# Scaling the probabilities of layer 1's attention on GpSimd instead of VectorE

## The chip, the cores and the metric

The kernel runs on one core of a Trainium2 chip, in one launch. The metric is the device time of a run in microseconds; lower is better. The core has TensorE (matrix products; the profile shows its weight loads as a unit of their own, PEld), VectorE (DVE), ScalarE (ACT), GpSimd (POOL) and SyncE (SP), each with its own stream of instructions, which meet in semaphores.

## The reference

The reference runs two blocks of two layers each over 256 positions of width 1024, with a second stream of 256 context positions in the first block. What matters here is layer 1 of the first block, a sliding-window attention with 16 query heads of 64 channels, 4 key heads, a context and a sink:

```python
def one_block(j):
    ...
    s_loc = jnp.einsum('bqkgd,bskd->bkgqs', q_blk, k_blk,
                       preferred_element_type=jnp.float32) * scale
    s_loc = jnp.where(valid, s_loc, NEG_INF)
    s_ctx = jnp.einsum('bqkgd,bckd->bkgqc', q_blk, kc,
                       preferred_element_type=jnp.float32) * scale
    s = jnp.concatenate([s_loc, s_ctx, s_sink], axis=-1)
    p = jax.nn.softmax(s, axis=-1).astype(v.dtype)
    return (jnp.einsum('bkgqs,bskd->bqkgd', p[..., :3 * T], v_blk)
            + jnp.einsum('bkgqc,bckd->bqkgd', p[..., 3 * T:3 * T + C], vc))
```

The softmax divides each row of exponentials by its sum; here that is done before the product with the values. Around it stand the normalisations, the projections, squared-ReLU layers of width 4096, and in the second block a state-space layer and a second attention.

## The kernel before

The whole network is one program with a function per engine. Most of the time goes into large products (`gemm` on TensorE, L730 to L732: three products for each pair of operands split into a high and a low part), whose weights SyncE loads in units of 512 KB. The stages stand one behind the other in every engine's program, in the same order: q1, k1, v1 of layer 1, its attention, its output projection wo1, and so on.

Layer 1's attention (`ATT1`) has 16 groups, each of two heads and 128 queries against 512 keys (256 positions and 256 of context). Group g uses two of four score banks, two of four `prob` tiles (g % 2 selects them) and one of four columns of `stat`, the small tile with maximum, sum, inverted sum and sink term. The steps of one group n are:

- scores (TensorE, L914): two heads, 64x128 against 64x512, into banks;
- mask (VectorE, L2120): the window, 256 keys wide, is added in the banks; maximum (L2121, a reduction over 128x1024); then two short steps for the sink (L2127, L2128);
- exponentials (ScalarE): L1436 for the sink term, L1440 twice into `prob`, each with a read of the accumulated row sum;
- sum (VectorE, L2136: row sum plus sink term), reciprocal (L2137), and the scaling of both heads' `prob` tiles in place (L2140, 128x512 f32 twice);
- transposes (TensorE, L925): four per head, each head once its tile is scaled;
- copy (ScalarE, L1427): both heads' transposed probabilities from the banks into `prob_t`;
- values (TensorE, L940): 16 small products into a bank; every second group its output goes to `u_hi` (ScalarE, L1448) and `u_lo` (VectorE, L2148).

The order on each engine is written out in its `attention` function. In step n TensorE does the scores of n+1, the transposes of n-1 and the values of n-2. VectorE does mask and maximum of n (`att_max`), sum, reciprocal and scaling of n-1 (`att_scale`), and the low part of the output of n-3. ScalarE does the copy of n-2, the output of n-3 and the exponentials of n. The scores of a group wait until the exponentials of the group two before it, which used the same banks, are done. The semaphore `att_r` counts scaled tiles: VectorE raises it after each head, and TensorE waits for it before that head's transposes. Layer 0's attention (`ATT0`) runs through the same functions with 32 groups, without sink and window, and its first 16 groups have the same shapes on TensorE.

GpSimd does no arithmetic here beyond a few memsets at the start. It issues DMAs: the rotated copies of queries and keys ahead of layer 1's attention (L2352), and behind it, once wo1's units are through, the table loads of `table_inputs` (L2316 to L2318) for the second block. Between the two it has nothing to do during layer 1's attention.

Of the kernel before, what the change touches and what calls it, by code (L numbers as in the profile page):

```python
# [7 lines left out]
ALU = mybir.AluOpType  # L8
# [9 lines left out]
TOK = 2 * SEQ  # L18
# [136 lines left out]
def program(nc, weights, ada_w, ada_b, x_t, vecs, cons, bias_na, ssm_in, ssm_bc, scratch, out):  # L155
# [5 lines left out]
    with ctx:  # L161
# [4 lines left out]
        def place(name, shape, dt=F32, at=None):  # L166
            size = int(np.prod(shape[1:])) * 4
            off = cursor[0] if at is None else at
            if at is None:
                cursor[0] += (size + 31) // 32 * 32  # L170
            return nc.alloc_sbuf_tensor_at(name, shape, dt, offset=off)
# [51 lines left out]
        prob = place("prob", [P, 4, TOK], at=at_)  # L223
# [4 lines left out]
        stat = place("stat", [P, 4, 4, 2], at=rsn_at)  # L228
# [85 lines left out]
        def sem(name):  # L314
            return ctx.enter_context(nc.semaphore(name))
# [34 lines left out]
        att_s, att_m, att_p, att_r, att_t, att_e, att_o, att_h, att_l = (sem("att_" + c) for c in (  # L350
            "scores", "max", "probs", "scaled", "transposed", "probs_t", "out", "out_hi", "out_lo"))
# [13 lines left out]
        ge_y, ge_t, ge_a, ge_sg, ge_g, ge_hi, ge_lo = (sem("gelu_" + c) for c in (  # L365
            "input", "square", "argument", "sigmoid", "product", "out_hi", "out_lo"))
        h_out = sem("h_out")

        block = ctx.enter_context(nc.Block())

        def value(name, s, n):

            return n + (CREDIT + s.base.get(name, 0))

        def stage_end(eng, s, names):

            inc = increments(s)
            for n in names:
                if n in inc:
                    eng.wait_ge(S[n], CREDIT + s.base.get(n, 0) + inc[n])  # L380

        class Chain:
# [13 lines left out]
            def link(self, ins):  # L396
                self.until(self.mark(ins))
# [44 lines left out]
        for s in ST.values():  # L442
            a = s.base.get("ada_read", 0)
# [71 lines left out]
        ATT0, ATT1 = [], []  # L515
# [1046 lines left out]
        def _(dve):  # L1562
# [445 lines left out]
            while n < CH:  # L2008
                b = [p_[:, n, :].unsqueeze(1).to_broadcast([P, n, PAIRS]) for p_ in (pr_, pi_)]
# [120 lines left out]
            def att_scale(groups, m, base):  # L2130
                _, keys, _, _, kind, _ = groups[m]
                g = m + base
                b = g % 4
                dve.wait_ge(att_p, 2 * g + 2)
                if kind == "swa":
                    link(TT(stat[:, 1, b, :], stat[:, 1, b, :], stat[:, 3, b, :], ALU.add))  # L2136
                link(dve.reciprocal(stat[:, 2, b, :], stat[:, 1, b, :]))  # L2137
                for a in range(2):
                    pb = prob[:, 2 * (g % 2) + a, 0:keys]
                    TS(pb, pb, stat[:, 2, b, a:a + 1], None, ALU.mult).then_inc(att_r, 1)  # L2140
# [140 lines left out]
        def _(pool):  # L2281
# [63 lines left out]
            for n, (name, done) in enumerate((("q1", 4), ("q1", 8), ("k1", 2))):  # L2345
                pool.wait_ge(S["d2"], value("d2", ST[name], done))
                if n == 0:
                    stage_end(pool, ST["down0b"], ("d1",))
                for p0 in range(0, P, 16):
                    p1 = p0 + 16 if p0 % 32 == 0 else p0 - 16  # L2350
                    src_ = q1[p1:p1 + 16, 4 * n:4 * n + 4, :] if n < 2 else k1[p1:p1 + 16, :, 0:SEQ]
                    pool.dma_start(turned[p0:p0 + 16, 4 * n:4 * n + (4 if n < 2 else 2), :], src_).then_inc(rope_in[n], 16)  # L2352
            stage_end(pool, ST["wo1"], ("unit",))
            table_inputs(HOME1, slice(PAIRS // 2, PAIRS))
            for n in range(4, PIECES):
# [169 lines left out]
```

## Time and profile before

| | |
|---|---|
| Median of 3 runs | 1713.21 us (1707.87 to 1715.15) |
| Span of the profiled execution | 1706.6 us |
| TensorE busy | 1606.4 us, 94% |
| Weight loads (PEld) busy | 1421.1 us, 83% |
| VectorE busy | 1308.7 us, 77% |
| ScalarE busy | 869.5 us, 51% |
| GpSimd busy | 104.3 us, 6% |
| Mean granted TensorE clock | 0.982 |

The profile is one execution, traced by the hardware; its span runs from the first to the last instruction. Times in the rows are microseconds from the span's start, durations are microseconds unless marked ns. Each instruction has its line in the kernel, and where its engine stood idle before it, the idle time and who ended it stand in square brackets. The ends of TensorE's instructions are modelled, so their starts say more than their durations. An arrow reads "written from".

### The profile page before, as it was taken

To read this page: it belongs to the slowest core of one execution; us is meant where nothing else is said; L and a number is where in the kernel's file an instruction comes from. 1 tells how busy PE (TensorE), PEld (TensorE's weight loads), DVE (VectorE), ACT (ScalarE), POOL (GpSimd) and SP (SyncE) were. 2 spreads that over 40 slices of the span, in tenths; PEclk is the share of its full clock that TensorE was granted. 3 is DMA by queue.
4 is the path that set the end of the run, shared out by engine and by line. 5 is a ranking of instruction groups with operands and counts; after the bars stand their busy time and mean duration, and the time that the engine had idled before them with its cause. 6 is when DMAs were issued, how large, how long until landed. Compare 5 with 4: busy or idle time off the path is not lost.

```text
span 1706.6 us, 32698 instructions
## 1 busy us (share of the span) xinstructions
PE 1606.4 (94%) x11872; PEld 1421.1 (83%) x11872; DVE 1308.7 (77%) x2229; ACT 869.5 (51%) x1505; POOL 104.3 (6%) x174
## 2 busy tenths in 40 slices
PE   6999899899999999788989999889999999899999
PEld 3778666688888888674789999789999998699999
DVE  5899897788767867678677787777887686578874
ACT  4664386343213433566555555355555586555542
POOL 0001030000000023120000212000000000000000
PEclk9999999999999999998999999999999999999999
DMA  9246651345667855340156667735555644055554
GB/s 368 89 137 224 218 149 51 123 144 184 202 193 238 263 173 169 112 140 12 53 186 202 217 208 263 316 102 176 179 183 177 205 153 158 13 164 183 182 196 137
DMA packets 80828, 292.02 MB, mean 171 GB/s; under 512 B 10432, under 2 KB 12224, under 8 KB 78928
## 3 DMA queue, kind: packets, MB, share of 16 engines
q1 hardware_dynamic: 69552, 249.03, 44.4%
q0 software_dynamic: 11168, 41.54, 7.6%
q8 instruction: 69, 1.13, 0.3%
q14 instruction: 39, 0.32, 0.1%
HBM read 270.54 MB, written 18.68 MB: 169 GB/s over the span
## 4 chain that ended last, share of the span: by engine, by line
PE 73%; DVE 18%; issue 4%; ACT 3%; DMA 2%; ACTq 0%; DVEq 0%; SPq 0%; POOLq 0%
PE bank L730 22%; PE bank L732 21%; PE bank L731 21%; DVE stat L2121 2%; DVE w_lo L1576 2%; DVE prob L2140 1%; PE bank L914 1%; DVE bank L1588 1%; DVE ada_raw L1589 1%; PE bank L925 1%; DMA raw<-weights 1%; PE bank L940 1%; DVE qk L1771 1%; DMA ada_raw<-ada_w 1%; PE bank L818 1%
## 5 line engine op out<-in xcount | busy, mean ns | idle before, releaser
L730 PE MATMUL bank<-u_hi,w_hi 128*128 128x256 f32 (+1 forms) x1936 | 615.9, 318 | 31.2 <-DVE u_lo L1951 19.2
L731 PE MATMUL bank<-u_lo,w_hi 128*128 128x256 f32 (+1 forms) x1936 | 600.8, 310 | 0.0
L732 PE MATMUL bank<-u_hi,w_lo 128*128 128x256 f32 (+1 forms) x1936 | 600.8, 310 | 0.0
L1576 DVE TENSOR_TENSOR w_lo<-raw,w_hi 128x1024 fp32r<-128x1024 f32 x372 | 452.2, 1222 | 143.9 <-ACT w_hi L1144 131.4
L1144 ACT ACTIVATE w_hi<-raw 128x1024 fp32r<-128x1024 f32 x360 | 375.4, 1049 | 172.8 <-PE bank L732 142.7
L730 PEld LDWEIGHTS bank<-u_hi,w_hi 128*128 128x128 f32 x1936 | 372.5, 192 | 59.6 <-issue 35.7
L731 PEld LDWEIGHTS bank<-u_lo,w_hi 128*128 128x128 f32 x1936 | 372.8, 193 | 22.3 <-issue 3.8
L732 PEld LDWEIGHTS bank<-u_hi,w_lo 128*128 128x128 f32 x1936 | 372.6, 192 | 18.4
L730 PE MATMUL bank<-hid_hi,w_hi 128*128 128x512 f32 (+1 forms) x512 | 174.0, 340 | 0.0
L732 PE MATMUL bank<-hid_hi,w_lo 128*128 128x512 f32 (+1 forms) x512 | 172.1, 336 | 0.0
L731 PE MATMUL bank<-hid_lo,w_hi 128*128 128x512 f32 (+1 forms) x512 | 172.0, 336 | 0.0
L730 PEld LDWEIGHTS bank<-hid_hi,w_hi 128*128 128x128 f32 x512 | 97.1, 190 | 11.0 <-issue 1.5
L732 PEld LDWEIGHTS bank<-hid_hi,w_lo 128*128 128x128 f32 x512 | 97.1, 190 | 10.2
L731 PEld LDWEIGHTS bank<-hid_lo,w_hi 128*128 128x128 f32 x512 | 97.1, 190 | 9.7
L1589 DVE SCALAR_TENSOR_TENSOR ada_raw<-ada_raw,silu_row 128x1024 f32<-128x1024 f32 x80 | 97.7, 1222 | 9.3 <-DMA ada_raw<-ada_w 9.0
L730 PE MATMUL bank<-f_hi,w_hi 128*128 128x256 f32 x352 | 99.8, 283 | 0.0
L731 PE MATMUL bank<-f_lo,w_hi 128*128 128x256 f32 x352 | 99.6, 283 | 0.0
L732 PE MATMUL bank<-f_hi,w_lo 128*128 128x256 f32 x352 | 99.6, 283 | 0.0
L1195 ACT ACTIVATE rs<-bank 128x512 f32<-128x512 f32 (+1 forms) x64 | 31.3, 489 | 125.2 <-PE bank L732 118.7
L730 PEld LDWEIGHTS bank<-f_hi,w_hi 128*128 128x128 f32 x352 | 67.6, 192 | 0.2
L732 PEld LDWEIGHTS bank<-f_hi,w_lo 128*128 128x128 f32 x352 | 67.6, 192 | 0.0
L731 PEld LDWEIGHTS bank<-f_lo,w_hi 128*128 128x128 f32 x352 | 67.6, 192 | 0.0
(317 smaller groups left out, 2260.3 us busy)
## 6 DMA issues: line engine op xcount, KB each, us to landing
raw<-weights SPq DMA_DIRECT2D x372, 512.0 KB, 3.4
ada_raw<-ada_w SPq DMA_DIRECT2D x80, 512.0 KB, 4.1
ada_first<-ada_w SPq DMA_DIRECT2D x16, 512.0 KB, 14.4
bias_sb<-bias_na POOLq DMA_DIRECT2D x16, 256.0 KB, 3.4
toep_dram<-zeros POOLq DMA_DIRECT2D x8, 512.0 KB, 9.1
bat_dram<-bat POOLq DMA_DIRECT2D x16, 256.0 KB, 4.2
ca_dram<-ca POOLq DMA_DIRECT2D x16, 256.0 KB, 3.8
s_bat<-bat_dram POOLq DMA_DIRECT2D x4, 1024.0 KB, 8.2
```

The lines of the kernel that those rows point to most:

```text
L730: pe.matmul(dst, wh, hi[:, kt, xs], start=first, stop=False)
L731: pe.matmul(dst, wh, lo[:, kt, xs], start=False, stop=False)
L732: return pe.matmul(dst, wl, hi[:, kt, xs], start=False, stop=final)
L818: pe.matmul(SUM_BANKS[b2][:, 0:s.tok], C("block"), sq[:, b2, 0:s.tok], start=True, stop=True).then_inc(S["p2"], 1)
L914: pe.matmul(psum[2 * (g % 2) + a][:, 0:keys], q_ap, k_ap, start=True, stop=True).then_inc(att_s, 1)
L925: mm = pe.transpose(psum[4 + a][:, t * P:(t + 1) * P], prob[:, 2 * (g % 2) + a, t * P:(t + 1) * P], C("ident"))
L940: mm = pe.matmul(psum[6 + pr % 2][a * HD:(a + 1) * HD, qt * P:(qt + 1) * P], heads[a][2][t], prob_t[:, 2 * (g % 2) + a, t * P:(t + 1) * P] ...
L1144: A(w_hi[:, slot, :], raw[:, slot, :], ACT.Copy).then_inc(S["hi"], 1)
L1195: chain.link(A(rs[:, b2, 0:s.tok], bank[:, 0:s.tok], ACT.Relu))
L1576: TT(w_lo[:, slot, :], raw[:, slot, :], w_hi[:, slot, :].bitcast(F32), ALU.subtract).then_inc(S["lo"], 1)
L1589: STT(raw_, raw_, 1.0, silu_row[:, 0, :], ALU.mult, ALU.mult, accum_out=ada_acc[:, b, a % 4, 0:1]).then_inc(S["ada_read"], 1)
L2121: red = dve.tensor_reduce(stat[:, 0, b, :], both[:, :, 0:keys], AX.X, ALU.max, negate=True)
```

## The change

After the reciprocal, VectorE's part of a group ends in layer 1 with a raise of a new semaphore `att_v`. GpSimd waits for it once per group, and then does the two scalings in place, with the same operands as VectorE had, and raises `att_r`. VectorE no longer waits for its own reciprocal there. Layer 0's attention stays as it was. In GpSimd's program the sixteen groups stand behind the DMAs of the rotated keys and ahead of the wait for wo1.

```diff
+        att_v = sem("att_sums_inverted")
...
                 if kind == "swa":
                     link(TT(stat[:, 1, b, :], stat[:, 1, b, :], stat[:, 3, b, :], ALU.add))
+                if kind == "swa":
+                    dve.reciprocal(stat[:, 2, b, :], stat[:, 1, b, :]).then_inc(att_v, 1)
+                    return
                 link(dve.reciprocal(stat[:, 2, b, :], stat[:, 1, b, :]))
                 for a in range(2):
                     pb = prob[:, 2 * (g % 2) + a, 0:keys]
...
+            for m in range(len(ATT1)):
+                g = m + len(ATT0)
+                pool.wait_ge(att_v, m + 1)
+                for a in range(2):
+                    pb = prob[:, 2 * (g % 2) + a, 0:TOK]
+                    pool.tensor_scalar(pb, pb, stat[:, 2, g % 4, a:a + 1], None, ALU.mult).then_inc(att_r, 1)
             stage_end(pool, ST["wo1"], ("unit",))
```

## Rows read from the trace of the kernel before

**Rows 1.** The page: the chain that ended last, shares of the span by engine and line.

```profile
PE 73%; DVE 18%; issue 4%; ACT 3%; DMA 2%; ACTq 0%; DVEq 0%; SPq 0%; POOLq 0%
PE bank L730 22%; PE bank L732 21%; PE bank L731 21%; DVE stat L2121 2%; DVE w_lo L1576 2%; DVE prob L2140 1%; PE bank L914 1%; DVE bank L1588 1%; DVE ada_raw L1589 1%; PE bank L925 1%; DMA raw<-weights 1%; PE bank L940 1%; DVE qk L1771 1%; DMA ada_raw<-ada_w 1%; PE bank L818 1%
```

**Rows 2.** Stretches of layer 1's attention: length, busy per engine, clock, DMA share, GB/s.

```profile
772.00:784.00 12.00, 9.81 (x26) 3.92 (x27) 8.23 (x21) 5.13 (x15) 0.00 (x0) 0.51 0.00 1
784.00:828.00 44.00, 40.00 (x360) 25.66 (x358) 40.69 (x110) 34.30 (x84) 0.00 (x0) 1.00 0.01 1
```

**Rows 3.** Timeline, layer 1's attention: start, duration, engine, line, operation, [idle before].

```profile
786.01 0.15 DVE L2136 TENSOR_TENSOR stat<-stat 128x2 f32<-128x2 f32 x1
...
789.26 0.15 DVE L2136 TENSOR_TENSOR stat<-stat 128x2 f32<-128x2 f32 x1
789.38 0.20 ACT L1436 ACTIVATE stat<-stat 128x2 f32<-128x2 f32 x1
789.45 0.17 DVE L2137 RECIPROCAL stat<-stat 128x2 f32<-128x2 f32 x1
...
789.65 0.88 DVE L2140 TENSOR_SCALAR prob<-prob,stat 128x512 f32<-128x512 f32 x2
...
790.19 1.09 PE L925 MATMUL bank<-con,prob 128*128 128x128 f32 x8
...
790.72 0.20 ACT L1440 ACTIVATION_READ_ACCUMULATOR prob<-bank,stat 128x1 f32 x1
...
791.22 1.09 PE L940 MATMUL bank<-prob_t,val 128*64 128x128 f32 x16
...
792.24 1.13 PE L914 MATMUL bank<-k,q 64*128 64x512 f32 x4
...
794.03 0.42 DVE L2120 TENSOR_TENSOR bank<-bank,con 128x256 f32<-128x256 f32 x1
...
796.10 0.15 DVE L2136 TENSOR_TENSOR stat<-stat 128x2 f32<-128x2 f32 x1
```

**Rows 4.** Timeline, layer 0's attention: GpSimd released by VectorE's maximum.

```profile
210.72 1.23 DVE L2121 TENSOR_REDUCE stat<-bank 128x2 f32<-128x1024 f32 x1
...
212.24 0.84 POOL L2304 DMA_DIRECT2D bias_sb<-bias_na  x1 [2.44 <-DVE stat L2121]
```

**Rows 5.** Waits from 784 to 828: who waited for whom, us, times, longest.

```profile
PEld bank L925 <- DVE prob L2140: 12.5, 12, 1.2
```

**Rows 6.** Timeline of TensorE in layer 0's attention: scores of two groups in succession.

```profile
211.82 1.13 PE L914 MATMUL bank<-qk 64*128 64x512 f32 x4
...
214.92 1.13 PE L914 MATMUL bank<-qk 64*128 64x512 f32 x4
```

**Rows 7.** GpSimd's memsets by line and form: count | busy us, mean ns | idle.

```profile
L2284 POOL MEMSET zeros<- 128x128 f32 x1 | 0.2, 223 | 0.0
L2512 POOL MEMSET const-float32-1.0<- 128x1 f32 x1 | 0.1, 99 | 0.0
```

**Rows 8.** Timeline, the last groups: sum and transposes of the last but one, its copy.

```profile
827.16 0.16 DVE L2136 TENSOR_TENSOR stat<-stat 128x2 f32<-128x2 f32 x1
...
828.10 1.09 PE L925 MATMUL bank<-con,prob 128*128 128x128 f32 x8 [1.47 <-DVE prob L2140]
...
829.28 1.02 ACT L1427 ACTIVATE prob_t<-bank 128x1024 f32<-128x1024 f32 x1 [0.46 <-issue]
```

**Rows 9.** Timeline: scores at the lower clock, and the mask that waited for them.

```profile
781.79 2.08 PE L914 MATMUL bank<-k,q 64*128 64x512 f32 x4
...
783.94 0.43 DVE L2120 TENSOR_TENSOR bank<-bank,con 128x256 f32<-128x256 f32 x1 [0.57 <-PE bank L914]
```

**Rows 10.** Timeline: the first group's sum and its transposes.

```profile
778.55 0.15 DVE L2136 TENSOR_TENSOR stat<-stat 128x2 f32<-128x2 f32 x1
...
779.89 1.97 PE L925 MATMUL bank<-con,prob 128*128 128x128 f32 x8
```

**Rows 11.** Timeline of GpSimd: its first instruction after layer 1's attention.

```profile
858.57 0.74 POOL L2316 DMA_DIRECT2D tab_bbar<-bbar_dram  x1 [92.41 <-PE bank L732]
```

## The prediction

> **What bounds the kernel now.** I read the page first. TensorE is busy for 94% of the span and holds 73% of the chain that ended last, nearly all of it in the big products of L730 to L732; VectorE's share of that chain is 18%, and one of its entries is L2140, the line that the change moves [rows 1]. An edit to VectorE pays only where the chain runs through VectorE, so I went to the one stage touched. By the busy times of three stretches, layer 1's attention has a start of 12 us with TensorE at a granted clock of 0.51, its lower level (1.2 GHz), after it had waited for the rotated keys, and then 44 us at 1.00 (2.4 GHz), in which VectorE is busy 40.69 us and GpSimd 0.00 [rows 2].
>
> The timeline of two consecutive groups shows the order [rows 3]. VectorE's sum of group n (L2136) starts at 789.26, the same instruction two groups on at 796.10: 6.84 us for two groups, 3.42 for one. From the sum that starts at 786.01 (group 2) to that of group 14 at 827.16 it is 41.15 us for twelve groups [rows 3, 8]: 3.43 each. In the table of waits TensorE's weight loads for the transposes (L925) wait 12.5 us for L2140 in this stretch [rows 5]. So VectorE sets the pace, and TensorE is close behind. How close shows layer 0's attention, whose later groups have the same shapes on TensorE: there scores start at 211.82 and the next scores at 214.92, and TensorE waits for nobody [rows 6]. That is 3.10 us per group, TensorE's own floor. Twelve groups at 3.10 are 37.2 us, so no version of this change that leaves TensorE alone can give back much more than 41.15 - 37.2 = 3.9 us, 0.23% of the run. The forecast lives or dies on whether GpSimd costs that little.
>
> **What is removed.** Per group two scalings on VectorE, 0.88 us together, from 789.65 [rows 3], and the short wait between the reciprocal and them. 16 groups x 0.88 = 14.1 us of VectorE time. VectorE's occupied time per group falls from 3.43 to about 2.5 us. That is not the gain, since the floor of 3.10 is late next, and since the scaled probabilities still have to be made before the transposes.
>
> **What is added.** Two scalings of 128x512 f32 on GpSimd, and a hop from VectorE to GpSimd. No row shows GpSimd doing arithmetic. The nearest are its two memsets: one element per partition takes 0.10 us, 128 elements 0.22 us [rows 7]. That is (0.223 - 0.099) / 127 = 0.98 ns per element, so 512 elements written cost 0.10 + 0.50 = 0.60 us by this slope. An operation that also reads can hide the reading under the writing (0.60) or do one after the other (0.10 + 1.00 = 1.10). I estimate 0.75 us for one scaling, T below: nearer to the memset, as it is the same engine with the same size of element, plus something for the read and the per-partition factor. If a third pass came in (reading, multiplying, writing, nothing overlapped), T would be 0.10 + 1.50 = 1.6; I keep 0.6 and 1.6 as the ends.
>
> The hop: where GpSimd waited for VectorE's maximum, the reduction ended at 211.95 and its next instruction began at 212.24, 0.29 us later; that one issues a DMA [rows 4]. VectorE's products reach TensorE within 0.10 (first scaling done near 790.09, transposes at 790.19) [rows 3]. I take 0.20 for the way in, between the two, and 0.10 for the way out.
>
> The Trainium skill, "GPSIMD Engine Reference", section Performance versus the Vector engine, gives one measured loop of 512 elements at 769 ns, and calls elementwise work on VectorE the rule, as GpSimd needs about twice its time. No trace here shows that figure yet; by it the result would be 0.3 us above my sum, and the rule speaks against this change.
>
> **The loop that carries the cost.** TensorE's order is written out: scores of group n+1, transposes of n-1, values of n-2. So this chain closes over two groups: sum of n, scaling of n, transposes of n, values of n-1, scores of n+3, mask, maximum and sink steps of n+3, sum of n+2. In rows [rows 3]: sum to transposes 789.26 to 790.19, 0.93; transposes to values 1.03; values to scores 1.02 (792.24); scores to the mask 1.20, being 1.13 of the scores and the 0.07 by which the mask at 783.94 follows the end of scores of 2.08 from 781.79, in a case where it did wait for them [rows 9]; mask to the next sum 794.03 to 796.10, 2.07. Together 6.25 per two groups, against 6.84 taken: 0.59 of slack, because VectorE is occupied.
>
> After the change the first two terms are rebuilt. Sum to the end of the reciprocal: 0.19 + 0.17 = 0.36 [rows 3]. Then the hop 0.20, two scalings 2T, out 0.10, and the second half of the transposes 0.51 (half of 1.03), since those of the second head can't start before its scaling is done. That is 1.17 + 2T where 0.93 + 1.03 = 1.96 stood. The loop becomes 1.17 + 2T + 1.02 + 1.20 + 2.07 = 5.46 + 2T per two groups. With T = 0.75 it is 6.96, or 3.48 per group: above the floor of 3.10, and 0.05 above now. From the sum of group 2 to that of group 14 it turns six times: 6 x 6.96 = 41.8 against 41.15, so +0.6 us. VectorE is then no longer full, and waits for scores in every group.
>
> I looked at the next loop too: exponentials of n, scaling, transposes, ScalarE's copy, exponentials of n+2, which share ScalarE. ScalarE's steps for the exponentials begin at 789.38 and end at 790.92, 1.54 [rows 3]; with sum and reciprocal 0.5, the hop, 2T, 0.10 + 0.51, and copies of 1.02 plus some 0.3 of hand-overs, it is about 4.2 + 2T = 5.7, below 6.96. It does not decide.
>
> **Start and end of the stage.** The first sum starts at 778.55 and its transposes at 779.89, after scores at half clock [rows 10]. GpSimd's first scaling would be done at 778.55 + 0.36 + 0.20 + 0.75 = 779.86, its second at 780.61, when the first head's four transposes (half of 1.97) are still running: the slow start hides it. I cost it at nothing; with T = 1.1 about 0.7 us would come out from under that cover. At the end nothing hides it: the last but one sum starts at 827.16, its transposes at 828.10, and ScalarE's copy of them (829.28) hangs on these, and on the copy the last group's transposes [rows 8]. They come 1.17 + 2T - 1.96 = 0.7 us later. Behind it stands layer 1's output projection, on TensorE; so this is paid in full.
>
> **The wait on GpSimd.** GpSimd's program now waits sixteen times, and what is queued behind are the table loads of L2316. They start at 858.57, released by TensorE [rows 11]; the last scaling would be over near 832. They lose nothing, and so nobody behind them. VectorE has no new wait. SP's queue isn't touched. The semaphore of the scaled probabilities is counted up as before, by another engine.
>
> **The sum.** +0.6 in the loop, +0.7 at the end: +1.3 us. The profiled span is 1706.6 us; the runs' median is 1713.21, so 6.6 us lie around the span or between executions, and I leave them. Span 1707.9, time 1713.2 + 1.3 = 1714.5 us. In general the change costs 6 x (5.46 + 2T) - 41.15 + (2T - 0.79) = 14T - 9.2 us: nothing at T = 0.66, -0.8 at 0.6, +6.2 at 1.1, +13.2 at 1.6. A measurement of this kernel can tell about 0.5%, 8.6 us, from no change; that needs T of 1.27.
>
> **Rivals.** (a) GpSimd is quick, T below 0.66: the loop falls under 6.84 and at T = 0.4 TensorE's floor of 3.10 decides; the time is 1709.3 to 1713.2. For it speaks the small memset slope, against it that a memset reads nothing. Chance 0.20.
>
> (b) Slower: one scaling takes over 1.27 us. Mechanism and place as in the loop; at 1.6 the loop takes 8.66, 4.33 per group, and the time is 1726.4. For it: no row shows GpSimd reading and multiplying, and the operation takes a factor per partition. Chance 0.13.
>
> (c) Slower: GpSimd and VectorE shut each other out of SBUF whenever both work. The scaling of n overlaps VectorE's mask of n+2 (L2120), which reads its window there. The mask would start when GpSimd ends, 0.56 + 2T after the sum, and the next sum 2.07 later: 2.63 + 2T per group. This is above today's 3.43 from T = 0.40 on; at 0.75 it is 4.13 per group, 12 x 4.13 - 41.15 = +8.4, and with the end +9.1: 1722.3. Against it: VectorE's long steps here work on banks, outside SBUF but for the window. Chance 0.06. The Trainium skill, "Perfetto Trace Analysis", section Optimizing Scalar/DVE Operations, states it: the two share an SBUF port, so moving work between them might not help. The Trainium skill, "SBUF — State Buffer", section Who interferes with whom, limits it to double-rate operations and those with two inputs in SBUF; by that only the short sink steps could collide, and nothing is added.
>
> (d) The first arithmetic instruction of GpSimd brings its code late, once, at 778.9, with little to hide behind. Its very first memset took the same 0.10 us as those after it would by their size [rows 7], so the rows speak for nothing of the kind. Chance of a visible case 0.03. The Trainium skill, "GPSIMD Engine Reference", section Instruction dispatch, has about 6 us for the first call of newly loaded code; by that it would be 1720.5.
>
> (e) TensorE idles longer per group, its granted clock falls to the 0.51 of the stage's start, and groups take what they took there (scores 2.08, transposes 1.97, values taken as equal to these: 6.0) [rows 9, 10]. Twelve groups would add some 31 us. In all of 784 to 828 the clock stayed at 1.00 with waits of up to 1.2 us for L2140 [rows 2, 5]. Chance 0.01.
>
> (f) The change doesn't do what it says, as VectorE's part in the pace lies elsewhere; then nothing moves. The chain runs through L2140 in every group [rows 1, 3], so 0.02.
>
> **How the numbers follow.** The forecast case, T from 0.66 to 1.27, has 0.55 (1713 to 1722, with 1714.5 the likeliest). Cases (b), (c) and (e) are slower by over 0.5%: 0.20, less a little for T near the point: 0.19. Faster by over 0.5% is beyond what the floor allows; I leave 0.04 for the spread of the runs, which went from 1707.9 to 1715.2. The rest is within 0.5%: 0.77. The range must hold case (a) and most of the forecast case, and reach to (c): 1708 to 1723. Outside are (b)'s upper part, (e), and odd draws.
>
> **What would show it.** In the profile after: GpSimd's scalings with a start-to-start distance near 0.75; sums two groups apart by about 7.0; transposes waiting for GpSimd instead of VectorE; VectorE waiting for scores before each mask; VectorE busy some 14 us less in total; the clock at 1.00 through the stage. The prediction is wrong if T is far from 0.75, if VectorE's operations grow longer beside GpSimd's, or if the first scaling comes late.

## The result, and the profile after

The changed kernel takes 1728.89 us (median of 4 runs, 1728.37 to 1729.7) against 1713.51 us before; the ratio is 1.0098 with a 95% interval of 1.0078 to 1.0118. It is slower by 15.4 us, about 1%, where I had forecast no change, and it lies outside my range. The profiled execution has a span of 1727.5 us.

The page after, busy times per engine and the chain that ended last, by engine and by line:

```profile
PE 1615.2 (94%) x11872; PEld 1426.4 (83%) x11872; DVE 1295.7 (75%) x2197; ACT 869.9 (50%) x1505; POOL 154.1 (9%) x206
...
PE 74%; DVE 16%; issue 4%; ACT 3%; DMA 2%; POOL 1%; ACTq 0%; DVEq 0%; SPq 0%; POOLq 0%
PE bank L731 22%; PE bank L733 21%; PE bank L732 21%; DVE w_lo L1577 2%; DVE stat L2122 2%; POOL prob L2362 1%; PE bank L915 1%; PE bank L926 1%; PE bank L941 1%; DVE bank L1589 1%; DVE ada_raw L1590 1%; DMA raw<-weights 1%; DVE qk L1772 1%; DMA ada_raw<-ada_w 1%; PE bank L819 1%
```

VectorE has 13.0 us less to do, GpSimd 49.8 us more, and GpSimd's L2362 stands in the chain where VectorE's scaling stood [rows 1]. (Lines have moved: TensorE's scores are L915, its transposes L926, values L941; VectorE's mask is L2121, its sum L2137.)

To find where the 15.4 us are I cut the stage in the same four places in both kernels: first scores, sum of group 2, sum of group 14, first product of wo1. Stretches of the kernel before, then of the one after (length, busy per engine, granted clock, DMA share, GB/s):

```profile
771.91:786.01 14.10, 11.91 (x50) 5.69 (x52) 10.07 (x25) 6.55 (x17) 0.00 (x0) 0.58 0.00 1
786.01:827.16 41.15, 37.99 (x336) 23.98 (x336) 38.08 (x103) 32.16 (x78) 0.00 (x0) 1.00 0.01 2
827.16:834.99 7.83, 5.30 (x65) 4.29 (x65) 3.55 (x12) 5.11 (x10) 0.00 (x0) 1.00 0.00 0
```

```profile
774.93:790.47 15.54, 12.24 (x36) 5.56 (x38) 8.30 (x20) 5.69 (x17) 6.22 (x4) 0.50 0.00 1
790.47:841.42 50.95, 40.34 (x340) 23.91 (x338) 29.13 (x79) 31.42 (x79) 37.28 (x24) 1.00 0.00 1
841.42:852.75 11.33, 7.91 (x80) 6.12 (x77) 1.86 (x8) 6.01 (x11) 6.18 (x4) 0.85 0.00 0
```

The stage went from 63.08 to 77.82 us, 14.7 us more, against 15.4 between the medians. (The two profiled spans differ by more, 1727.5 against 1706.6. The other 6.2 us lie ahead of the stage and behind it, 3.0 and 3.1, where the change touches nothing; the stage starts at 771.5 to 776.1 in the profiles of the kernels below, so I take the 6.2 for spread between executions.) Of the 14.7, 1.4 lie in the start, 9.8 in the twelve groups, 3.5 at the end. In the middle VectorE is busy 29.1 of 51 us, so it no longer sets the pace, yet the stretch is longer. One turn of the loop after, from the sum of group 2 to that of group 4 (timeline):

```profile
790.47 0.15 DVE L2137 TENSOR_TENSOR stat<-stat 128x2 f32<-128x2 f32 x1
...
790.66 0.17 DVE L2139 RECIPROCAL stat<-stat 128x2 f32<-128x2 f32 x1
790.92 3.11 POOL L2362 TENSOR_SCALAR prob<-prob,stat 128x512 f32<-128x512 f32 x2 [2.25 <-DVE stat L2139]
...
794.09 0.66 PE L926 MATMUL bank<-con,prob 128*128 128x128 f32 x4 [0.89 <-POOL prob L2362]
...
794.67 1.09 PE L941 MATMUL bank<-prob_t,val 128*64 128x128 f32 x16
...
795.70 1.13 PE L915 MATMUL bank<-k,q 64*128 64x512 f32 x4
...
796.90 0.43 DVE L2121 TENSOR_TENSOR bank<-bank,con 128x256 f32<-128x256 f32 x1 [0.24 <-PE bank L915]
...
798.97 0.15 DVE L2137 TENSOR_TENSOR stat<-stat 128x2 f32<-128x2 f32 x1
```

The chain is the one of the forecast, and each link has the length it had in rows 3, but for the first. Sum to values 4.20 (before 0.93 + 1.03 = 1.96), values to scores 1.03, scores to mask 1.20, mask to sum 2.07: 8.50 us per two groups, against 6.84 [rows 3]. The mask now waits for the scores, which it didn't at 794.03 [rows 3]. The two scalings take 3.11 us together: 1.56 each, where I had put 0.75.

Who waits for whom between the sums of groups 2 and 14, after (us in total, times, longest), which answers rows 5:

```profile
PEld bank L926 <- POOL prob L2362: 23.0, 24, 1.1
...
POOL prob L2362 <- DVE stat L2139: 14.6, 12, 2.2
DVE bank L2121 <- PE bank L915: 11.4, 12, 1.7
```

Three engines wait in a ring: TensorE for GpSimd, GpSimd for VectorE's reciprocal, VectorE for TensorE's scores. No one of them is full: in the 50.95 us of the middle TensorE is busy for 40.3, GpSimd for 37.3, VectorE for 29.1.

### The profile page after: what moved, and what is told of

Its sections match the earlier page's. It is cut to its first block, busy times and chain, and to the rows that moved or that the text cites. A ratio compares the mean times of both kernels' runs of the same rounds, so it can differ in the third digit from the quotient of the medians.

```text
span 1727.5 us, 32700 instructions
## 1 busy us (share of the span) xinstructions
PE 1615.2 (94%) x11872; PEld 1426.4 (83%) x11872; DVE 1295.7 (75%) x2197; ACT 869.9 (50%) x1505; POOL 154.1 (9%) x206
## 3 DMA queue, kind: packets, MB, share of 16 engines
q8 instruction: 69, 1.13, 0.3%
## 4 chain that ended last, share of the span: by engine, by line
PE 74%; DVE 16%; issue 4%; ACT 3%; DMA 2%; POOL 1%; ACTq 0%; DVEq 0%; SPq 0%; POOLq 0%
PE bank L731 22%; PE bank L733 21%; PE bank L732 21%; DVE w_lo L1577 2%; DVE stat L2122 2%; POOL prob L2362 1%; PE bank L915 1%; PE bank L926 1%; PE bank L941 1%; DVE bank L1589 1%; DVE ada_raw L1590 1%; DMA raw<-weights 1%; DVE qk L1772 1%; DMA ada_raw<-ada_w 1%; PE bank L819 1%
## 5 line engine op out<-in xcount | busy, mean ns | idle before, releaser
L731 PEld LDWEIGHTS bank<-hid_hi,w_hi 128*128 128x128 f32 x512 | 97.1, 190 | 11.1 <-issue 1.5
L926 PEld LDWEIGHTS bank<-con,prob 128*128 128x128 f32 x320 | 36.4, 148 | 49.7 <-POOL prob L2362 28.6
```

The source lines that it names most:

```text
L731: pe.matmul(dst, wh, hi[:, kt, xs], start=first, stop=False)
L926: mm = pe.transpose(psum[4 + a][:, t * P:(t + 1) * P], prob[:, 2 * (g % 2) + a, t * P:(t + 1) * P], C("ident"))
```

## The experiments

Theory A throughout: the stage turns by that ring, whose length per two groups is a constant plus 2T, T being GpSimd's time for one scaling. Its rivals: GpSimd and VectorE shut each other out of SBUF; the hop itself is dear; GpSimd's throughput, or a loop over ScalarE, decides. All times below stand beside runs of the kernel before on the same chip, whose median there was 1710.5 to 1711.4 us. Sums are measured as in the profile after: from group 2's to group 14's, divided by six.

### What one operation of GpSimd costs (e1_probe)

```diff
+            pool.wait_ge(att_s, 2 * 32 + 4)
...
+            for _ in range(3):
+                probe(pool.tensor_scalar(sp_(0, 512), sp_(0, 512), con[:, 0:1], None, ALU.mult))
+                probe(pool.tensor_scalar(sp_(0, 256), sp_(0, 256), con[:, 0:1], None, ALU.mult))
+                probe(pool.tensor_scalar(sp_(0, 128), sp_(0, 128), con[:, 0:1], None, ALU.mult))
+                probe(pool.tensor_scalar(sp_(1, 512), sp_(1, 512), 1.5, None, ALU.mult))
+                probe(pool.tensor_copy(sp_(2, 512), sp_(1, 512)))
+                probe(pool.tensor_tensor(sp_(2, 512), sp_(0, 512), sp_(1, 512), ALU.mult))
+                probe(pool.memset(sp_(2, 512), 1.0))
```

> The kernel before, with GpSimd measuring itself beside layer 1's attention: from the third group on it runs, three times over and each waiting for the one before, scalings of 128x512, 128x256 and 128x128 f32 by a per-partition factor, a scaling of 128x512 by a constant, a copy, a product of two tiles and a memset of 128x512, all in spare tiles that nobody waits for. VectorE does its own scalings (L2140) at the same time. Theory A (the step costs about 3 ns per element whoever else works): 1.56 us at 512, 0.85 at 256, 0.5 at 128, in a straight line; VectorE's scalings stay at 0.48 each and the total time within 2 us of before. Theory B (the 1.56 us come from VectorE and GpSimd shutting each other out of SBUF): the durations scatter, the shortest at 512 lies near 0.75, and VectorE's L2140 or L2120 grow beside it. Theory C (the per-partition factor is what costs): the scaling by a constant takes about half of that by a factor.

1713.13 us, ratio 1.0015 (1.0005 to 1.0025), 2.6 above before by both: a little more than theory A allowed. GpSimd's operations by line and form (busy us, mean ns of one | idle before):

```profile
L2368 POOL TENSOR_SCALAR spare<-spare,con 128x512 f32<-128x512 f32 x3 | 4.7, 1565 | 0.3
L2371 POOL TENSOR_SCALAR spare<-spare 128x512 f32<-128x512 f32 x3 | 4.5, 1488 | 0.3
L2373 POOL TENSOR_TENSOR spare<-spare 128x512 f32<-128x512 f32 x3 | 4.0, 1331 | 0.3
L2369 POOL TENSOR_SCALAR spare<-spare,con 128x256 f32<-128x256 f32 x3 | 3.2, 1058 | 0.3
L2372 POOL COPY spare<-spare 128x512 f32<-128x512 f32 x3 | 2.2, 739 | 0.2
L2370 POOL TENSOR_SCALAR spare<-spare,con 128x128 f32<-128x128 f32 x3 | 1.8, 602 | 0.3
L2374 POOL MEMSET spare<- 128x512 f32 x3 | 1.6, 524 | 0.2
```

The 1.56 us are GpSimd's own: 1.56 in the ring, 1.56 or 1.57 in all three rounds here, with different work of VectorE beside it. So theory B does not explain T. Theory C falls as well: a constant in place of the factor saves 0.08. My extrapolation from the memsets was good for a memset (0.60 expected, 0.52) and, by luck, for a copy (0.75, 0.74), where the read adds 0.22 us to the memset. What I had no row for is the scaling itself. It costs 0.8 us over the copy, and more than a product of two tiles. That isn't the price of multiplying as such: a product against one repeated element does the same arithmetic in 1.04 us (f5_tt below). Why the scaling is dearer, no run shows. Widths of 128 and 512 take 0.60 and 1.56 us. The 1.06 us here for 256 stand beside VectorE's own scaling in all three rounds; undisturbed, in e2_half below, that width takes 0.92. So the line is straight, as theory A had it, but with some 0.3 us ahead of 2.5 ns per element (an estimate from 0.60, 0.92 and 1.56).

The Trainium skill, "GPSIMD Engine Reference", section Engine selection, calls operations with one input roughly line-rate and puts the two-input ones at twice VectorE's time. The scaling does not fit: it has one tile as its input, yet is slower than the product of two, and takes 3.2 times VectorE's 0.48. The copy takes 1.5 times that 0.48; VectorE's own copy or product at this width is in no run.

Theory B has something in it all the same, which I come back to below: VectorE did not come through undisturbed. Here are a sink step that takes 0.16 alone, the GpSimd scaling that began just ahead of it, and VectorE's two scalings, 0.88 alone (timeline):

```profile
786.14 1.56 POOL L2368 TENSOR_SCALAR spare<-spare,con 128x512 f32<-128x512 f32 x1
786.22 0.62 DVE L2131 TENSOR_TENSOR stat<-stat,neg_sink 128x2 f32<-128x2 f32 x1
...
787.14 1.45 DVE L2143 TENSOR_SCALAR prob<-prob,stat 128x512 f32<-128x512 f32 x2
```

The next pairs of VectorE's scalings took 1.24, 1.19 and 1.24 us, beside GpSimd's copy or its scaling of 256. Theory B's first sign, durations that scatter down to 0.75, failed; its second, that VectorE's scalings grow, came true, and the twelve groups took 43.10 us instead of 41.15.

### Less of it: half the columns, and a cheaper operation (e2_half, f5_tt)

```diff
-                    pb = prob[:, 2 * (g % 2) + a, 0:TOK]
+                    pb = prob[:, 2 * (g % 2) + a, 0:SEQ]
```

> The changed kernel, with GpSimd scaling only the first 256 of the 512 columns of each tile; the other 256 are left unscaled, so their values aren't the reference's. Theory A (the stage turns by the loop 5.46 + 2T per two groups): with T near 0.85 the sum of L2137 comes every 3.58 us instead of 4.25, the time is 12 to 14 us below the changed kernel and 1 to 4 us above before. Rival (a fixed cost of the hop to GpSimd and back is what slows the stage): the time falls by less than 6 us from the changed kernel.

1714.55 us, ratio 1.0020 (1.0010 to 1.0029), 14.3 below the changed kernel's median, 13.3 by the two ratios. Sums 7.21 us apart per two groups, 3.60 for one, where theory A had 3.58; the two scalings of 256 columns take 1.82 us.

```diff
-                    pool.tensor_scalar(pb, pb, stat[:, 2, g % 4, a:a + 1], None, ALU.mult).then_inc(att_r, 1)
+                    pool.tensor_tensor(pb, pb, stat[:, 2, g % 4, a:a + 1].to_broadcast([P, TOK]), ALU.mult).then_inc(att_r, 1)
```

> The changed kernel, but GpSimd scales with a product of two tiles, the second being the inverted sum read 512 times, in place of the scaling by a per-partition factor. If the duration seen beside the attention (1.33 against 1.56 us) carries over, the two groups take 2 x 0.23 = 0.46 us less, 8.03, and the time is 2.5 to 3.5 us below the changed kernel's. Rival (reading one element over and over is as slow or slower): no gain.

1716.35 us, ratio 1.0033 (1.0021 to 1.0045), 12.5 below the changed kernel's median, 11.1 by the two ratios. The gain is far more than the 2.5 to 3.5 expected, as the product against a repeated element takes 1.04 us, not 1.33; two take 2.04. Sums 7.41 us apart. The middle and the end, cut as above:

```profile
790.15:834.59 44.44, 39.90 (x338) 23.87 (x336) 29.13 (x80) 32.05 (x79) 24.46 (x24) 1.00 0.01 1
834.59:843.59 9.00, 5.60 (x67) 4.25 (x65) 2.41 (x8) 5.23 (x11) 4.08 (x4) 1.00 0.00 0
```

With the changed kernel that makes three points for the loop. GpSimd's time for a group and the time of two groups: 3.11 and 8.49 (50.95 / 6), 2.04 and 7.41, 1.82 and 7.21. The difference is 5.38, 5.37 and 5.39. The ring's constant is 5.38 us, and each microsecond of scaling is paid in full. The rival of a fixed cost of the hop is out, since nothing but T was changed.

### One head for each engine (e4_split, g1_tt_split)

GpSimd raises a semaphore of its own, `att_q`, for which TensorE waits ahead of the second head's transposes.

```diff
                     dve.reciprocal(stat[:, 2, b, :], stat[:, 1, b, :]).then_inc(att_v, 1)
+                    dve.wait_ge(att_v, m + 1)
+                    pb = prob[:, 2 * (g % 2), 0:keys]
+                    TS(pb, pb, stat[:, 2, b, 0:1], None, ALU.mult).then_inc(att_r, 1)
                     return
...
+                pb = prob[:, 2 * (g % 2) + 1, 0:TOK]
+                pool.tensor_scalar(pb, pb, stat[:, 2, g % 4, 1:2], None, ALU.mult).then_inc(att_q, 1)
```

> The changed kernel, but VectorE scales the first head's tile of each group and GpSimd the second's, side by side, with a semaphore of its own. Theory A: from sum to values 0.36 + 0.09 + 1.56 + 0.06 + 0.51 = 2.58 us, the loop 6.87 per two groups, so 3.43 for one, just what the kernel before takes; time within 2 us of before (+0.6). Rival (both at once in SBUF lock each other out): VectorE's scaling grows from 0.44 towards 2 us, and the time lies at least 5 us above before.

1714.34 us, ratio 1.0027 (1.0016 to 1.0038): 3.8 us above before by the medians, 4.6 by the ratio, between the two theories. Sums 7.24 us apart, not 6.87. The timeline shows both engines starting on their head:

```profile
802.39 0.49 DVE L2145 TENSOR_SCALAR prob<-prob,stat 128x512 f32<-128x512 f32 x1
802.45 1.86 POOL L2367 TENSOR_SCALAR prob<-prob,stat 128x512 f32<-128x512 f32 x1 [2.08 <-DVE stat L2142]
```

VectorE's scaling has its usual length; GpSimd's takes 1.86 in place of 1.56 us. GpSimd lost 0.30 us. With 1.86 for GpSimd's part the ring gives 5.38 + 1.86 = 7.24, as measured. So the loop held and the price was off, by waiting that I had ascribed to neither side.

In g1_tt_split GpSimd's operation is the product of f5_tt; the rest is as above.

```diff
-                pool.tensor_scalar(pb, pb, stat[:, 2, g % 4, 1:2], None, ALU.mult).then_inc(att_q, 1)
+                pool.tensor_tensor(pb, pb, stat[:, 2, g % 4, 1:2].to_broadcast([P, TOK]), ALU.mult).then_inc(att_q, 1)
```

> One head scaled by VectorE, the other by GpSimd with the product against the inverted sum read 512 times, which took 1.04 us; order as before. With 0.3 us of waiting for VectorE's scaling: sum to values 0.36 + 0.07 + 1.34 + 0.06 + 0.60 = 2.43, the loop 6.72 per two groups against 6.86 in the kernel before. Theory A: within 1.5 us of before, either way. Rival (GpSimd's product and VectorE's scaling hinder each other more, as both read two streams): VectorE's scaling grows beyond 0.6, 3 us slower.

1719.61 us, ratio 1.0046 (1.0030 to 1.0061). Here the rival is right:

```profile
800.01 1.37 DVE L2145 TENSOR_SCALAR prob<-prob,stat 128x512 f32<-128x512 f32 x1
800.05 1.04 POOL L2367 TENSOR_TENSOR prob<-prob,stat 128x512 f32<-128x512 f32 x1 [2.69 <-DVE stat L2142]
```

Now GpSimd has its usual 1.04 and VectorE's scaling takes 1.37 in place of 0.48 us, 0.9 us more, which I read as waiting; it ends 0.29 after GpSimd does. VectorE is then occupied 3.43 - 0.88 + 1.37 = 3.9 us per group, is the bound again, and the sums stand 7.80 us apart (46.80 / 6). The faster operation made the slower kernel: by the ratios' intervals that isn't quite clear of noise, but the stage is 71.04 us here against 66.41 in e4_split. The Trainium skill, "SBUF — State Buffer", section Who interferes with whom, says that a double-rate operation of VectorE and one of GpSimd block each other for a whole instruction. Whether VectorE's scaling is such an operation, no run here shows. The times agree nearly for g1_tt_split, where VectorE's scaling ends 0.29 us after GpSimd's 1.04 are over. They agree less for e4_split, where GpSimd lost 0.30 beside an operation of 0.49. The sink step of e1_probe, another kind of operation, ended 0.70 us after GpSimd's scaling began, 0.86 before that was over.

### A quarter for GpSimd (e7_quarter)

VectorE also scales the second head's first 256 columns, and GpSimd the other 256. The edit is shown against e4_split.

```diff
+                    pb = prob[:, 2 * (g % 2) + 1, 0:256]
+                    TS(pb, pb, stat[:, 2, b, 1:2], None, ALU.mult).then_inc(att_r, 1)
...
-                pb = prob[:, 2 * (g % 2) + 1, 0:TOK]
+                pb = prob[:, 2 * (g % 2) + 1, 256:TOK]
```

> VectorE scales the first head's tile and the first 256 columns of the second's, GpSimd the last 256 columns of the second's; the last two transposes of the second head wait for it. Order as in the kernel before. From sum to values 0.36 + 0.09 + 0.9 to 1.2 + 0.06 + 0.26, at most 1.97, as before: the loop doesn't lengthen (6.26 at most per two groups), and VectorE is occupied about 0.2 us less per group. Theory A: 3.2 to 3.3 us per group, 1.5 to 2.5 us faster than before. Rival (GpSimd's start makes VectorE's scaling wait or the reverse): VectorE's second scaling grows by 0.3 us or more, and nothing is gained.

Ratio 1.0006 (0.9994 to 1.0017), no difference. Sums 7.03 us apart, a little more than the 6.86 before. GpSimd's operation takes 1.22 us (0.92 undisturbed), and VectorE's second scaling, 256 wide, 0.57 us where that width takes 0.35 in layer 0. What VectorE gave away came back as waiting.

### TensorE's order (e3_order, f1_late, f2_late_split, g2_tt_late_split, f4_late_only)

These take the values out of the ring, by placing them behind the next scores:

```diff
-                att_scores(groups, 0, base)
-                for n in range(n_g + 2):
-                    if n + 1 < n_g:
-                        att_scores(groups, n + 1, base)
+                att_scores(groups, 0, base)
+                if base:
+                    att_scores(groups, 1, base)
+                for n in range(n_g + 2):
+                    if not base and n + 1 < n_g:
+                        att_scores(groups, n + 1, base)
                     if 0 <= n - 1 < n_g:
                         att_transpose(groups, n - 1, base)
+                    if base and n + 2 < n_g:
+                        att_scores(groups, n + 2, base)
                     if 0 <= n - 2 < n_g:
                         att_values(groups, n - 2, base)
```

> The changed kernel, but in layer 1's attention TensorE does the scores of n+2 ahead of the values of n-2, right behind the transposes of n-1. GpSimd's work is the same. Theory A (the loop through scaling, transposes, values, scores, mask carries the cost): the values' 1.02 us leave the loop, 8.59 becomes 7.57 per two groups, 3.79 for one; the time is 5 to 6.5 us below the changed kernel's (about 1723). Rival (GpSimd's throughput of 3.1 us per group and waits around it set the pace, or the loop over ScalarE's exponentials does): under 2 us of change.

A miss, and on the other side: 1736.45 us, ratio 1.0152 (1.0135 to 1.0169), sums 10.0 us apart. The timeline says why (ScalarE's and VectorE's lines are 4 further down than in the changed kernel):

```profile
804.53 1.52 PE L941 MATMUL bank<-prob_t,val 128*64 128x128 f32 x16
...
806.09 0.39 ACT L1453 ACTIVATE u_hi<-bank 128x256 fp32r<-128x256 f32 x1 [2.39 <-PE bank L941]
...
806.51 0.42 DVE L2156 TENSOR_TENSOR u_lo<-bank,u_hi 128x256 fp32r<-128x256 f32 x1 [5.44 <-ACT u_hi L1453]
806.85 0.42 DVE L2125 TENSOR_TENSOR bank<-bank,con 128x256 f32<-128x256 f32 x1
```

In every second group ScalarE's output step waits for the values, with the exponentials queued behind it, and VectorE's waits for ScalarE's, with the mask queued behind it. I had moved the values out of one ring and into two others. TensorE's clock adds to it: it was granted 0.91 on the mean of the twelve groups, against 1.00 in the changed kernel. f1_late has the same order, and both output steps one group later:

```diff
-                    if 0 <= n - 3 < n_g:
-                        att_out_hi(groups, n - 3, base)
+                    back = 4 if base else 3
+                    if 0 <= n - back < n_g:
+                        att_out_hi(groups, n - back, base)
```

> The changed kernel with TensorE's values of n-2 behind the scores of n+2, and, unlike the run before of that order, ScalarE's and VectorE's output steps (L1448 and L2148 of the kernel before) one group later, so that neither engine waits for the values ahead of its exponentials or its mask. Theory A (the loop from sum to sum): 4.19 from sum to values becomes 4.19 from sum to the scores, and the loop is 4.19 + 1.20 + 2.07 = 7.46 us per two groups instead of 8.49; the time is 5 to 7 us below the changed kernel's. Rival (what made the former order slow is the order itself, or the loop over ScalarE's exponentials, about 7.1 to 8.5): the same as the changed kernel, or slower.

1723.98 us, ratio 1.0076 (1.0059 to 1.0093), 4.9 below the changed kernel's median, 3.8 by the two ratios, which is a little short of the 5 to 7 expected: the end of the stage grew from 11.3 to 13.3 us. Sums 7.73 us apart instead of 8.49, where 7.46 was expected: three quarters of the gain, with GpSimd's work untouched. So it is the ring that costs, not GpSimd's throughput of 3.1 us per group. The missing quarter comes up again under f2_late_split.

The other three join edits already shown: f2_late_split is e4_split, g2_tt_late_split is g1_tt_split and f4_late_only is the kernel before, each with the order and the outputs of f1_late.

> One head scaled by VectorE and the other by GpSimd, and TensorE's order and the output steps as in f1_late. GpSimd's operation takes 1.86 us beside VectorE's. Loop: sum to scores 2.95, then 1.20 + 2.07: 6.22 per two groups, 3.11 for one, at TensorE's floor of 3.10; VectorE is occupied 3.0. Theory A: 3.1 to 3.2 per group, 2 to 4 us faster than before. Rival (the short loop over ScalarE: copy, exponentials, reciprocal): 3.4 or more per group, no gain.

Ratio 1.0011 (1.0002 to 1.0020): sums 6.69 us apart, less than before's 6.86, but the expected 6.22 and the gain of 2 to 4 us did not come. The twelve groups are 1.0 us shorter than before, and the end, at 9.51 us, 1.7 longer.

Sum by sum both runs start as expected and then slow down. In f2_late_split the first two groups after the sum at 790.29 take 6.22 us, the last eight 6.82 to 6.84 per two; in f1_late the first six take 7.46 or 7.47 per two, the last four 8.07 and 8.08. The trace has a second ring for the slow turns. It runs over every second group's output steps, from a sum to the sum two groups on (f2_late_split, timeline):

```profile
807.07 0.15 DVE L2145 TENSOR_TENSOR stat<-stat 128x2 f32<-128x2 f32 x1
...
807.52 1.85 POOL L2373 TENSOR_SCALAR prob<-prob,stat 128x512 f32<-128x512 f32 x1 [2.12 <-DVE stat L2147]
...
809.43 0.66 PE L929 MATMUL bank<-con,prob 128*128 128x128 f32 x4 [0.40 <-POOL prob L2373]
...
810.17 1.02 ACT L1435 ACTIVATE prob_t<-bank 128x1024 f32<-128x1024 f32 x1 [1.27 <-issue]
...
811.50 0.42 DVE L2163 TENSOR_TENSOR u_lo<-bank,u_hi 128x256 fp32r<-128x256 f32 x1 [0.70 <-ACT u_hi L1456]
811.84 0.42 DVE L2129 TENSOR_TENSOR bank<-bank,con 128x256 f32<-128x256 f32 x1
...
813.90 0.15 DVE L2145 TENSOR_TENSOR stat<-stat 128x2 f32<-128x2 f32 x1
```

GpSimd's scaling is followed by the transposes, ScalarE's copy, the output on ScalarE and VectorE, and the mask queued behind it. From the sum to GpSimd's start it is 0.45 us, from its end to the transposes 0.06, to the copy 0.74, to VectorE's part of the output 1.33, to the mask 0.34, to the next sum 2.06. That makes 4.98 us plus GpSimd's time: 6.83 with 1.85, as measured, and 8.09 with f1_late's 3.11, against 8.07 and 8.08. No run took the output steps out of it, so this is read from the traces and not tried.

> As g1, with TensorE's values behind the scores of n+2 and the outputs one group later. The loop of the sums would be 5.70, below TensorE's floor of 6.20 per two groups; the same order with the slower operation came to 6.69. Theory A: 6.2 to 6.5 per two groups, 2 to 4 us faster than before, the fastest kernel of this study. Rival (in this order a loop over ScalarE's copy and exponentials decides, whatever GpSimd takes): 6.7, no difference from before.

1716.75 us, ratio 1.0036 (1.0023 to 1.0049), sums 7.74 us apart. Neither theory: VectorE's scaling takes 1.36 us here as in g1_tt_split, VectorE is occupied about 3.9 us per group, and the order can't help. I had written this expectation, like that of g1_tt_split, with 0.3 us of waiting on GpSimd's side.

> The kernel before with TensorE's order and the later outputs alone; all scaling on VectorE. Theory A (VectorE is occupied 3.43 us per group, whatever the order): sums 6.8 to 6.9 us apart for two groups, the time within 1 us of before. Rival (the order was a limit of its own): 6.2 to 6.5, 2 to 4 us faster.

Ratio 1.0002 (0.9992 to 1.0012), sums 6.80 us apart. With VectorE scaling, the order is worth nothing: before was bound by VectorE, as the forecast has it.

### The start and the end (g3_middle)

GpSimd scales groups 2 to 13 only, VectorE the first two and the last two.

```diff
-                if kind == "swa":
+                if kind == "swa" and 2 <= m < 14:
                     dve.reciprocal(stat[:, 2, b, :], stat[:, 1, b, :]).then_inc(att_v, 1)
...
-            for m in range(len(ATT1)):
+            for m in range(2, 14):
```

> The changed kernel, but GpSimd scales only groups 2 to 13 of layer 1; the first two and the last two stay with VectorE, in the kernel before's way. In the changed kernel's profile the stage is 14.7 us longer than before: 9.8 between the sums of groups 2 and 14, 1.4 ahead of them and 3.5 behind. Theory A (start and end are the exposed scalings of the first and last groups): the 1.4 goes, and most of the 3.5; the time is 4 to 5 us below the changed kernel's, with the sums in between still 8.5 us apart for two groups. Rival (start and end are longer because of TensorE's clock or something else that comes with GpSimd's work in between): under 2 us of it goes.

1722.77 us, ratio 1.0073 (1.0054 to 1.0092), 6.1 below the changed kernel's median, 4.3 by the two ratios. The stretches, with the middle cut in two:

```profile
772.44:786.49 14.05, 11.86 (x50) 5.70 (x52) 10.07 (x25) 6.56 (x17) 0.00 (x0) 0.58 0.00 1
786.49:806.59 20.10, 16.09 (x114) 9.29 (x114) 9.72 (x28) 10.72 (x26) 12.42 (x8) 0.83 0.01 1
806.59:840.55 33.96, 26.42 (x226) 15.87 (x224) 19.42 (x53) 21.45 (x53) 24.86 (x16) 1.00 0.00 1
840.55:848.38 7.83, 5.32 (x66) 4.28 (x65) 3.54 (x12) 5.21 (x11) 0.00 (x0) 1.00 0.00 0
```

Start and end are back at 14.05 and 7.83 us, the lengths of before. So the 1.4 and the 3.5 came with the scalings of the first and the last groups; what part of them is the clock, this run can't tell. The eight groups from 806.59 on take 33.96 us, 8.49 per two, as expected. The four ahead of them take 20.1, 10.05 per two: TensorE's clock, 1.00 there before, has a mean of 0.83, so it was at its lower level in part of them: the scores at 792.40 and 802.36 took 2.08 us instead of 1.13. The twelve groups take 54.06 us for it, 3.1 more than in the changed kernel, which takes back part of what start and end give. In this one execution the stage is 1.9 us shorter than the changed kernel's (75.94 against 77.82); the rest of the 4.3 or 6.1 lies outside it, where executions differ by as much.

## Why the prediction was wrong

**The failed step is the price of one scaling.** I estimated T at 0.75 us, near the memset, with 0.6 and 1.6 as ends; it is 1.56. The formula that I worked out, 14T - 9.2, gives 12.6 us for it, or 1725.8; measured were 15.4, and 14.7 in the stage. The 2.1 us between are 1.4 at the start, 1.2 more than its term at the end, and 0.5 less in the loop. The upper end that I had for T, three passes with nothing overlapped, was the right size, but for no good reason: in e1_probe the copy takes only 0.22 us more than the memset, so three passes in a row are not what makes 1.56. Rival (b), slower by a scaling over 1.27 us, is what happened; I gave it 0.13. An operation that no row shows, on an engine that does no arithmetic in the whole trace, deserved wider odds, and my range ended at 1723, below the 1726.4 that I had worked out for the upper end of T myself.

**The loop** was right in every link. 5.46 + 2T was 5.38 + 2T, at three values of T. The 0.08 is three small misses: GpSimd starts 0.09 after the reciprocal's end, not 0.20, TensorE 0.06 after GpSimd's, not 0.10, and the second head's transposes take 0.58 to the values (794.09 to 794.67), not 0.51.

**The end** was right as 2T - 0.79, as long as the clock held: 1.17 us measured in f5_tt (9.00 - 7.83) for 1.25, and in e2_half 0.95 for 1.04. In the changed kernel it gives 2.3, and 3.5 were measured, with the clock at 0.85 in that stretch. TensorE's steps after the last but one sum show where it was low (timeline):

```profile
845.03 1.12 PE L926 MATMUL bank<-con,prob 128*128 128x128 f32 x4 [0.88 <-POOL prob L2362]
846.08 1.97 PE L941 MATMUL bank<-prob_t,val 128*64 128x128 f32 x16
```

They took 0.66 and 1.09 us at 1.00, so some 1.3 us are the clock's, and that is the 1.2 beyond the term.

**The start**, costed at nothing with 0.7 as its price at T = 1.1, took 1.4: at T = 1.56 the cover of the slow transposes is gone. My own 0.7 plus twice the 0.46 makes 1.6. The first group's second four transposes began 3.64 us after its sum (at 785.21), against some 2.3 before (1.34 and half of 1.97, rows 10). I had seen this term and left it out of the formula.

**Rival (a)** is out. **Rival (c)**, the lock-out, is not what slowed the changed kernel: between the sums of groups 2 and 14 VectorE's mask takes 0.43 and its sink steps 0.16 us, as before. The mask runs beside GpSimd's scaling (at 792.49) and is not longer for it. The sink steps, at 794.22 and 794.48, fall into GpSimd's pause from 794.03 to 795.00. The lock-out is real, though, where both scale at once, and it took the gain from e4_split, e7_quarter and g1_tt_split. **Rival (d)** is out: the trace has a configuring step of GpSimd's queue, 12.8 us ahead of the first scaling, and that starts at 782.03, 0.10 after its reciprocal, in its usual 1.57 us.

```profile
L2362 POOLq MODIFY_POOL_CONFIG  x2: 37/37/37, 769.2 to 769.2; - x2
```

**Rival (e)** was there in small: the clock stayed at 1.00 in the twelve groups, but 0.50 against 0.58 in the start and 0.85 against 1.00 at the end. It accounts for the 1.2 us at the end, and for little in the start, where 1.3 of the 1.4 us are the later transposes. This is read from the traces, not tried by itself. **Rival (f)** is out: GpSimd's L2362 stands in the chain of the page after.

**VectorE's relief** came as forecast (13.0 us busy for 14.1), and was worth nothing: the time that it no longer worked, it waited for the ring (11.4 us for the scores alone).

What stays open: why GpSimd's scaling is dearer than its product, who waits when VectorE and GpSimd scale at once, and what lowers TensorE's clock in g3_middle, but not in the same groups of the changed kernel. The second ring, over the output steps, is not tried. No kernel of the study beats the one before.

## What to carry to other kernels

Relieving the busiest engine pays only down to the next limit (here 3.9 us in all, by the forecast's estimate), while the new engine's latency is paid in full if the moved step lies in a ring of waits; so find the ring, write its length as a constant plus the moved operation's time, and see from which time on it loses. When that time is in no row, measure the operation first, in spare tiles beside the running kernel, as e1_probe does, and don't extrapolate from a memset. Shortening one ring shows the next, as f1_late and f2_late_split did. Before splitting work between VectorE and GpSimd, look at whether both would then be in SBUF at the same moment.

## What the runs showed of the hardware

- One GpSimd operation on 128x512 f32 takes 0.52 us as a memset, 0.74 as a copy, 1.04 as a product with one repeated element, 1.33 as a product of two tiles, and 1.56 as a scaling by a per-partition factor. The scaling takes 0.60 at 128 columns and 0.92 at 256.
- Beside VectorE's scaling (0.48 us), GpSimd's scaling grew by 0.30 us and VectorE's not at all (e4_split); with GpSimd's product, which began at the same point, it was VectorE's that grew, by 0.89 (g1_tt_split). VectorE's began first in both, by 0.06 and 0.04 us. Whether the form or those hundredths decide who waits, no run shows.
- From the end of VectorE's reciprocal to GpSimd's operation it is 0.07 to 0.10 us, from the end of the maximum to GpSimd's DMA issue 0.29 [rows 4], and from GpSimd's scaling to TensorE's transposes 0.06.
- TensorE's clock can fall back to its lower level in groups in which it stayed at 1.00 in the kernel before and in the changed one: 0.83 over 20 us in g3_middle, after waits of 1.12 and 0.90 us for GpSimd.
